# The transpose of the hidden activations moves from VectorE to TensorE in a two-layer decoder trunk

## The reference, cut to what matters

```
D_MODEL = 1024; SEQ = 256; D_FF = 2816; MACARON_WEIGHT = 0.5

def swiglu(h, wg, wu, wd):
    return (jax.nn.silu(h @ wg) * (h @ wu)) @ wd

def sandwich(x, pre, post, fn, weight):
    return x + weight * rms_norm(fn(rms_norm(x, pre)), post)

# each layer:
#   x = sandwich(x, ffn1_pre, ffn1_post, swiglu(wg, wu, wd), 0.5)
#   x = sandwich(x, mix_pre,  mix_post,  mixer,               1.0)
#   x = sandwich(x, ffn2_pre, ffn2_post, swiglu(wg, wu, wd), 0.5)
```

## Time and profile before

| what | value |
|---|---|
| median of 3 runs | 1021.66 us (1020.84 to 1022.58) |
| the profiled execution's own time | 1021.66 us |
| its span, first to last instruction | 1019.9 us |
| PE busy | 988.8 us, 97% |
| PEld busy | 824.5 us, 81% |
| DVE busy | 804.0 us, 79% |
| ACT busy | 496.3 us, 49% |
| POOL busy | 66.1 us, 6% |
| mean granted TensorE clock | 0.992 |
| read from HBM | 176.41 MB, 174 GB/s |

### The profile page before, as it was taken

One profiled execution on the slowest core, in us unless ns is written; L12 is line 12 of the kernel. 1 busy time (PEld: TensorE's weight loads), 2 busy tenths in 40 slices (PEclk: granted clock), 3 DMA queues, 4 the chain that ended last, 5 costly groups with the idle time before them and its releaser, 6 DMA issues.

```text
span 1019.9 us, 13682 instructions
## 1 busy us (share of the span) xinstructions
PE 988.8 (97%) x4755; PEld 824.5 (81%) x4755; DVE 804.0 (79%) x1537; ACT 496.3 (49%) x775; POOL 66.1 (6%) x112
## 2 busy tenths in 40 slices
PE   7999999999899999999999999999989899999997
PEld 5788888888778888888888888878878788888886
DVE  4888878756878897887889887876558769888784
ACT  6254353666655435344635435466356553543533
POOL 6000000132001000000200000030000011000000
PEclk9999999999999999999999999999989999999999
DMA  9556746432084575657276574726700364557442
GB/s 311 196 195 198 247 147 224 150 134 84 31 280 159 192 247 174 196 203 249 64 246 207 167 244 150 266 90 225 252 11 2 104 199 152 193 180 245 153 134 83
DMA packets 127411, 178.13 MB, mean 175 GB/s; under 512 B 3154, under 2 KB 102596, under 8 KB 127364
## 3 DMA queue, kind: packets, MB, share of 16 engines
q1 hardware_dynamic: 122832, 170.90, 50.3%
q10 hardware_dynamic: 4020, 6.33, 1.8%
q0 software_dynamic: 512, 0.28, 0.1%
HBM read 176.41 MB, written 1.09 MB: 174 GB/s over the span
## 4 chain that ended last, share of the span: by engine, by line
PE 90%; DVE 5%; ACT 1%; issue 1%; DMA 1%; SPq 1%; DVEq 0%; POOLq 0%; ACTq 0%; POOL 0%
PE ps L959 87%; DVE w_lo L1363 1%; PE ps L1143 1%; PE ps L996 1%; DMA raw<-in_l_ffn_wu 1%; PE ps L972 1%; DVE ps L1463 1%; DVE xt_lo L1375 0%; SPq L412 0%; DVE raw_down L1589 0%; DVE h L1586 0%; DVE raw L1395 0%; DVE heads L1395 0%; SPq L432 0%; ACT w_hi L672 0%
## 5 line engine op out<-in xcount | busy, mean ns | idle before, releaser
L959 PE MATMUL ps<-w_hi,xt_hi 128*128 128x512 f32 (+2 forms) x912 | 355.3, 390 | 8.0 <-DVE w_lo L1363 3.4
L959 PE MATMUL ps<-w_hi,xt_lo 128*128 128x512 f32 (+2 forms) x912 | 352.5, 387 | 0.0
L959 PE MATMUL ps<-w_lo,xt_hi 128*128 128x512 f32 (+2 forms) x912 | 352.1, 386 | 0.0
L1363 DVE TENSOR_TENSOR w_lo<-raw,w_hi 128x2048 fp32r<-128x2048 f32 (+3 forms) x118 | 259.0, 2233 | 56.0 <-ACT w_hi L672 55.9
L672 ACT ACTIVATE w_hi<-raw 128x2048 fp32r<-128x2048 f32 (+3 forms) x118 | 214.9, 1868 | 9.3 <-DMA raw<-in_l_w_in 6.1
L1463 DVE STREAM_TRANSPOSE ps<-h 32x128 f32<-32x128 f32 x640 | 206.6, 323 | 9.4
L959 PEld LDWEIGHTS ps<-w_hi,xt_hi 128*128 128x128 f32 x912 | 171.7, 188 | 44.8 <-issue 6.0
L959 PEld LDWEIGHTS ps<-w_hi,xt_lo 128*128 128x128 f32 x912 | 171.6, 188 | 34.9
L959 PEld LDWEIGHTS ps<-w_lo,xt_hi 128*128 128x128 f32 x912 | 171.8, 188 | 33.6
L762 ACT ACTIVATE ht_hi<-ps 128x512 fp32r<-128x512 f32 x40 | 24.0, 599 | 290.3 <-DVE ps L1463 281.1
L959 PE MATMUL ps<-down_hi,ht_hi 128*128 128x512 f32 x320 | 124.9, 390 | 1.4 <-DVE down_lo L1483 1.4
(11 more groups left out here) (190 smaller groups left out, 832.2 us busy)
## 6 DMA issues: line engine op xcount, KB each, us to landing
raw_down<-in_l_ffn_wd SPq DMA_DIRECT2D x44, 1024.0 KB, 5.0
raw<-in_l_ffn_wg SPq DMA_DIRECT2D x42, 1024.0 KB, 7.3
raw<-in_l_ffn_wu SPq DMA_DIRECT2D x42, 1024.0 KB, 9.8
raw<-in_l_w_in SPq DMA_DIRECT2D x7, 2048.0 KB, 9.0
raw<-in_l_w_out SPq DMA_DIRECT2D x4, 2048.0 KB, 8.3
gpost<-in_l_ffn_post ACTq DMA_DIRECT2D x4, 512.0 KB, 5.2
bias<-bias_rows ACTq DMA_DIRECT2D x1, 2048.0 KB, 10.1
raw<-in_l_nsa_wk SPq DMA_DIRECT2D x1, 2048.0 KB, 8.5
```

What stands on the lines that cost most here:

```text
L959: return pe.matmul(dst, lhs, rhs, start=start, stop=stop, skip_group_check=True)
L1363: dve.tensor_tensor(part(w_lo), part(raw), part(w_hi).bitcast(F32), ALU.subtract).then_inc(main_lo, 1)
```

## The change

`turn_h` moves from DVE's program to PE's. There it turns a block of `h` with four transposes of 128x128 (2 chunks of channels x 2 tiles) against the identity, in place of DVE's 16 instructions. For block 0 it stands between the two tiles of `gate_up(1)`; for blocks 1 to 9 it stands right behind `down(jc - 1)`. The semaphore `down_used` and ACT's wait for it are gone: `ht_ready` now comes from PE behind `down(jc - 1)`, so it says the same. The layer's last block, the mixers, the splits and the DMAs are as before.

```diff
@@ ACT, turned_h
                     act.wait_ge(ht_ready, g(d0 + jc + 1, 1))
-
-                    if u * (FBLOCKS - 1) + jc >= 1:
-                        act.wait_ge(down_used, g(u * (FBLOCKS - 1) + jc, 1))
                     act.activation(ht_hi[:, :, :], ...)
@@ PE, ffn
+                def turn_h(jc, g):
+                    pe.wait_ge(h_ready, g(2 * (d0 + jc) + 2, 2))
+                    if d0 + jc >= 1:
+                        pe.wait_ge(ht_l, g(d0 + jc, 1))
+                    for c in range(FC):
+                        for t in range(TILES):
+                            at = c * SEQ + t * P
+                            ins = pe.transpose(ps[:, 6, at:at + P], h[:, t, c * P:(c + 1) * P], ident[:, :])
+                    ins.then_inc(ht_ready, 1)
...
-                gate_up(1, fixed)
+                gate_up(1, fixed, between=lambda: turn_h(0, fixed))
                 down(0, fixed)
+                turn_h(1, fixed)
                 gate_up(2, fixed)
                 down(1, fixed)
+                turn_h(2, fixed)
                 with pe.Fori(0, (FBLOCKS - PEEL) // 2 - 1) as i:
                     for q in range(2):
...
                         gate_up(PEEL + q, looped)
                         down(PEEL + q - 1, looped)
+                        turn_h(PEEL + q, looped)
                 gate_up(FBLOCKS - 2, fixed)
                 down(FBLOCKS - 3, fixed)
+                turn_h(FBLOCKS - 2, fixed)
@@ DVE, ffn
-                def turn_h(jc, g):
-                    dve.wait_ge(h_ready, g(2 * (d0 + jc) + 2, 2))
-                    if d0 + jc >= 1:
-                        dve.wait_ge(ht_l, g(d0 + jc, 1))
-                    turned = ps[:, 6, :].rearrange("p (c t r) -> p t c r", c=FC, t=TILES)
-                    rows = h[:, :, :].rearrange("p t (c r) -> p t c r", c=FC)
-                    for q in range(4):
-                        for b in range(4):
-                            ins = dve.transpose(turned[32 * b:32 * b + 32, :, :, 32 * q:32 * q + 32],
-                                                rows[32 * q:32 * q + 32, :, :, 32 * b:32 * b + 32])
-                    ins.then_inc(ht_ready, 1)
...
                     mul(jc, 1, g)
-                    turn_h(jc, g)
```

More of the change, by code:

```diff
@@ L294, in trunk @@
         ht_ready, ht_h, ht_l = sem("ht_ready"), sem("ht_h"), sem("ht_l")
-        down_used = sem("down_used")
         rows_step = sem("rows_step")
@@ L1072, in down @@
                         for t in tiles:
-                            ins = rows_product(jc, t, part, usual)
-                    if TILES - 1 in tiles:
-                        ins.then_inc(down_used, 1)
+                            rows_product(jc, t, part, usual)
                 def down_end(t, part):
```

## The result

The changed kernel took 1036.91 us (1036.31 to 1038.38), the one before 1021.98 us beside it; the ratio is 1.0153 (1.0141 to 1.0166). It is slower, as forecast, and 1.3 us under the forecast of 1038.2: inside the range of 1036 to 1041.5, and just under the 1037 that was the lower bound of the sum. The profiled execution took 1038.06 us, 16.4 more than the one of before, at a mean granted clock of 0.994.

What follows compares the result with a forecast made beforehand. The prediction took PE to bound the kernel in the feed-forward layers. Transposes at +18.2 us and the removed first-layer stall at -1.6 gave +16.6 on 1021.66, a forecast of 1038.2 us, range 1036 to 1041.5.

Steps and rivals of the forecast that it cites:

- What bounds it: In the feed-forward layers PE sets the time; sparing DVE shortens nothing except where PE stands still.
- The transposes on PE, +18.2: Four PE transposes a block at 0.455 us, in 40 blocks, add 18.2 us (17.8 to 18.3).
- The stall at `down(0)`, -1.6: First layer: PE's wait for `down_lo` before `down(0)` goes, giving -1.6 us (bounds -1.6 to 0).
- Rival 1: PE really waits for `h_ready` before the transposes, at block 1 above all: up to 3.6 us more, 1042; chance 0.05.
- The argument for block 1: DVE's chain to block 1's product starts 0.9 us sooner, so PE's wait is 0, with a margin of 1.1 us.
- The zero: The added waits for `h_ready` in front of the transposes count 0 in all blocks, bounds 0 to 3.6 us.
- Rival 2: Loop branch and register instructions show behind the short transposes: up to 5.4 us more, 1044; chance 0.07.
- Rival 3: PE's transposes don't overlap, each costs its full 0.271 us: 43.4 less 1.6, 1063; chance 0.01.
- Rival 4: DVE's transposes slow PE's matmuls beside them, so without them the time is 1021.7 us or less; chance 0.03.
- The sum: The transposes' +18.2 and the stall's -1.6 make +16.6 us on 1021.66, forecast 1038.2 us.

Runs made afterwards that it cites:

- copy_only: The kernel before, with DVE's 16 transposes of a block replaced by one DVE copy and the turn left out; 1017.88 us, ratio 0.9971.
- first_on_pe: The kernel before, with only block 0 of the first layer turned on PE, the other 39 blocks on DVE; 1018.76 us, ratio 0.9981.
- both_turn: The changed kernel, with 16 DVE transposes a block added back, writing to SBUF that nobody reads; 1039.97 us, ratio 1.0184.
- pe_twice: The changed kernel, with every group of four PE transposes issued twice; 1052.44 us, ratio 1.0323.

## Why the prediction was right

- **What bounds it.** PE does. But for the one stall, DVE at 79% lay wholly beside PE in the feed-forward layers, and copy_only shows it: 161.18 us for the layer's 711 matmuls against 161.21. (The 5.37 us a block are from the first transpose's start to the last one's end; 16 at 323 ns are 5.17.)
- **The transposes on PE, +18.2.** The mechanism was right, the size 1 us too small. Forecast 0.455 us a group, measured 0.475 to 0.48 (40 x 0.48 = 19.2). I had measured the four of the earlier trace rows only up to the second matmul behind them, at 747.88, and the tail lies behind that. The same trace holds the better number seven matmuls further on:

```profile
749.49 0.39 PE L959 MATMUL ps<-w_hi,xt_lo 128*128 128x512 f32 x1
```

That is the ninth matmul behind the group. From 746.97 to there are 2.52 us, less nine distances (2.04) is 0.48. The eight of the earlier trace rows were cut off at the second matmul in the same way.
- **The stall at `down(0)`, -1.6.** Right. The gap is gone after the change, in first_on_pe, copy_only and rows_later, and back in both_turn. `ht_hi` began at 33.41, where 33.9 was forecast, in an execution whose layer began 0.4 us sooner.
- **Rival 1, a real wait for `h_ready`.** It didn't happen in the changed kernel. The argument for block 1 (its chain shifts by 0.9 us) held for the second layer, where I had made it: the product is over at 332.03 and PE comes to it at 333.17, a margin of 1.1 us, as forecast. For the first layer I made none, and there both_turn pays 1.2 us. The zero was right for the first layer only because DVE was relieved.
- **Rival 2, the loop's edge.** Refuted: 16.80 us outside the loop and 16.81 across its branch.
- **Rival 3, serial transposes.** Refuted by the four-more of pe_twice, 0.107 each.
- **Rival 4, DVE's transposes slow PE.** Refuted by copy_only, and by the changed kernel itself, where 72 matmuls take 16.36 us or more without DVE's transposes and took 16.325 with them.
- **The sum.** +17.6 by the measured terms (19.2 - 1.6), where +14.9 and +16.75 us were measured by medians. The mis-sized term and this shortfall lie in opposite directions, so that the total came within 1.3 us of the forecast is in part luck. In the profiled pair the shortfall is in the mixers (-0.8 us) and the start (-0.4 us), which differ between executions of one kernel too. In microseconds the two intervals are 14.4 to 17.0 and 15.8 to 19.0, so the second holds 17.6 and the first ends just under it; the difference between them isn't explained further.

## What to carry to other kernels

An engine that is busy 79% beside one that is busy 97% may have next to nothing to give, here one stall of 1.6 us: first find the places where the late engine really stands still, and price only those. Work that is moved onto the engine that sets the time costs its full issue distance, small as it looks beside the engine that it leaves: here 0.48 us for 5.37 us. And where one stall is all that there is to win, look for an order that removes it; moving the bias rows won about 2 us (1.1 to 3.3 by the interval) with no work moved between engines.

## What the runs showed of the hardware that was not expected

- A 128x128 transpose on PE lasts 0.271 us by its record and adds 0.107 us in a row of them. Behind a group the plain matmuls are 0.23 to 0.24 us apart for about ten of them, not 0.227, which is 0.03 us a group in the changed kernel.
- A stall of PE of 3 us was followed in three of four cases by the granted clock at 0.50 (1.2 GHz), beginning between the first matmul and 1 us behind it, and 8 to 12 matmuls then took 1.6 to 2.6 us more. In two of the three most of that would have been lost in a wait for DVE anyway.
- The granted clock fell without a change of the program, too: two profiles of the changed kernel differ in the first mixer (1.00 there in one, 0.59 and 0.56 in the other). In the first microseconds of the first layer it was at 0.50 in some kernels' profiles and at 1.00 in others', as these windows (us, busy time of PE, PEld, DVE, ACT and POOL, then the clock) of copy_only and of pe_twice show, one after the other:

```profile
22.00:24.00 2.00, 2.00 (x6) 1.51 (x6) 2.00 (x2) 2.00 (x4) 1.62 (x1) 0.50 1.04 370
```

```profile
22.00:24.00 2.00, 2.00 (x10) 1.65 (x9) 2.00 (x3) 2.00 (x4) 1.50 (x1) 1.00 1.04 375
```

Eight matmuls at 0.43 in place of 0.23 us are 1.6 us, so a few such stretches are most likely the 2 to 4 us by which executions of one kernel differ. The 40 runs of the kernel before bear it out: the 14 with a mean granted clock of 0.995 or more took 1018.23 to 1019.76 us, the 26 with 0.994 or less 1020.40 to 1022.36 us. No run varied the clock by itself.
